# Low-rank decay product of a GLA layer moved out of the kernel's first phase, with row sums per token

## Chip, cores and metric

One core of one Trainium2 chip. The metric is device microseconds of one execution of the whole program, the median of several; lower is better.

## The reference, cut to what matters

Two blocks of layers on x (256 tokens, 1024 features, fp32). Only the entrance of the first block matters here: an RMS norm, one wide product with w_in, whose columns are split among several consumers, and a gated linear attention (GLA) whose decay comes from 16 of these columns (ha) through a second small product.

```python
def rmsnorm(x, g):
    xf = x.astype(jnp.float32)
    y = xf * lax.rsqrt(jnp.mean(xf * xf, axis=-1, keepdims=True) + EPS)
    return (y * g.astype(jnp.float32)).astype(x.dtype)

h = rmsnorm(x, ln1[i])
hq, hk, hv, hr, ha, hatt, hgate = _split_cols(h @ w_in[i], SPLIT_SIZES)
log_a = jax.nn.log_sigmoid((ha @ w_a2[i] + b_a[i]).astype(jnp.float32)) / GLA_TAU
o = gla_mixer(hq.reshape(B, S, GLA_HEADS, GLA_DK), hk.reshape(B, S, GLA_HEADS, GLA_DK),
              hv.reshape(B, S, GLA_HEADS, GLA_DV), log_a.reshape(B, S, GLA_HEADS, GLA_DK))
```

Behind it come dilated attention, gates, an MLP, and a second block with gated feed-forward layers, a convolution and latent attention.

## The kernel before, in words

The program is a list of phases, one for each weight matrix (or part of one). A phase has groups of 256 output columns; a group has blocks of four 128-row pieces of the weight, 512 KB each. SP loads the blocks in order into a ring of eight (`raw`). Each value is held as a high part (rounded to the format that TensorE multiplies at full pace) and the rest: ACT rounds a block five ahead of TensorE (`round_block`, L1006, "cast"), DVE forms the rest four ahead (`rest_block`, L1284), and TensorE multiplies high with high and low (`high`, L606, 512 columns) and low with high (`low`, L612, 256 columns). For x the same two parts lie in `xa`.

The results of group G stand in one of two accumulator banks (`ps`), bank G % 2. Behind a group ACT copies the half with the small terms (`take_lohalf`, L1034, "half copy"), DVE adds it to the other half (L1334, `val`), and only then may TensorE start group G + 2 (`val_done`). DVE scales by the norm afterwards (`keep`), so that the products need not wait for the norm.

Each engine runs its own list, written out by hand in program order: for each group first `ahead` (casts, rests), then the group's evacuation, then the steps that tables put there. `GLA_AT` is such a table: it names behind which group each GLA step runs (z, log, cum, q', kdec, scores, upd0, upd2, o, on0, on1, oT, og), and it holds for TensorE, ACT and DVE alike. Other steps are tied to fixed groups: `angles` (sine and cosine of the positions; DVE at att_k2 group 0, ACT at att_k2 group 1, `sine_and_cosine` on DVE at att_v2 group 0), and `small_inputs` (ACT issues the DMAs of gains and small tables).

Before, the first phase is "ha": 128 columns of w_in of which 16 are used, three products of 256 columns for each piece (L654), as its width is not one of the wide phases. TensorE first transposes x (L690), ACT copies it out (L1142), DVE splits it (`split_gained`, L1299, L1302), ACT squares it (L1050), and TensorE sums the squares over the features with a matrix of ones (`input_sum`, L711). ACT's root and DVE's reciprocal give the norm; then come the issues of `small_inputs` (L1157 to L1164), the groups of gla_q, and behind them the norm turned to one value per token, the gains turned (L690) and the relative bias (L728).

## Time and profile before

| | us |
|---|---|
| median of three runs | 1505.89 |
| lowest, highest | 1505.78, 1507.74 |
| span of the profiled execution | 1504.7 |
| TensorE busy in it | 1483.5 |
| DVE busy | 1139.9 |
| ACT busy | 746.9 |
| GpSimd busy | 39.5 |

The profile is of one execution; its times run from the first to the last instruction, and the runs' time has a little more around it. TensorE's busy time counts matmuls whose ends are modelled, so small waits do not show in it; they are read from the order in time. "PE" is TensorE, "PEld" its weight load, "POOL" GpSimd, and ACTq the issue of a DMA by ACT. A matmul with plain fp32 operands has two records.

### The profile page before, as it was taken

What the parts mean: (1) busy time and instruction counts of PE and PEld (TensorE: products, weight loads), DVE (VectorE), ACT (ScalarE), POOL (GpSimd) and SP (SyncE); (2) the same over time, 40 slices, a digit from 0 to 9 for tenths busy, and PEclk for the clock granted to TensorE, in tenths of its full rate; (3) what the DMA queues carried; (4) which work ended last, traced back from release to release, by engine and by line L of the source; (5) the groups of instructions that cost most, each with busy time, mean ns of one, the idle gap of its engine ahead of it and who ended that gap; (6) DMA issues with size and microseconds to landing.
All of it is one profiled execution on the core that took longest, in us unless ns stands there. A gap on an engine that the chain in (4) does not pass through costs nothing.

```text
span 1504.7 us, 25207 instructions
## 1 busy us (share of the span) xinstructions
PE 1483.5 (99%) x9770; PEld 1331.1 (88%) x9770; DVE 1139.9 (76%) x1521; ACT 746.9 (50%) x1011; POOL 39.5 (3%) x77
## 2 busy tenths in 40 slices
PE   8999999999999999999999999999999999999997
PEld 6889899998898988888986888999888998888887
DVE  6777866789865688787876877678776788887754
ACT  5645456545434375544544645445553444555443
POOL 1000000200000000000121000000000000000000
PEclk9999999999999999999999999999999999999999
DMA  7636665456655566645632666567664664466553
GB/s 224 188 114 180 190 178 159 151 184 191 186 187 190 162 189 184 193 154 186 217 112 66 189 185 193 156 189 217 184 192 155 194 171 154 127 184 192 164 171 113
DMA packets 268919, 260.12 MB, mean 173 GB/s; under 512 B 15702, under 2 KB 267172, under 8 KB 268826
## 3 DMA queue, kind: packets, MB, share of 16 engines
q1 hardware_dynamic: 266832, 255.89, 56.4%
q0 software_dynamic: 1072, 1.98, 0.5%
q8 instruction: 64, 1.05, 0.3%
q10 hardware_dynamic: 922, 0.97, 0.2%
q14 instruction: 29, 0.24, 0.1%
HBM read 257.73 MB, written 1.07 MB: 172 GB/s over the span
## 4 chain that ended last, share of the span: by engine, by line
PE 93%; DVE 4%; ACT 1%; issue 1%; DMA 0%; DVEq 0%; ACTq 0%
PE ps L606 43%; PE ps L612 22%; PE ps L654 22%; PE misc L868 2%; PE misc L690 1%; PE misc L822 1%; PE misc L813 1%; DVE wsplit L1284 0%; PE misc L843 0%; PE misc L686 0%; DVE plain L1360 0%; PE misc L711 0%; DVE val L1334 0%; DMA plain<-in_x_dram 0%; PE misc L772 0%
## 5 line engine op out<-in xcount | busy, mean ns | idle before, releaser
L1284 DVE TENSOR_TENSOR wsplit<-raw,wsplit 128x1024 fp32r<-128x1024 f32 (+2 forms) x532 | 584.7, 1129 | 104.2 <-ACT wsplit L1006 93.9
L1006 ACT CAST wsplit<-raw 128x1024 fp32r<-128x1024 f32 (+2 forms) x532 | 494.5, 968 | 174.8 <-DMA raw<-in_ffn_w_dram 85.1
L606 PE MATMUL ps<-xa,wsplit 128*128 128x512 f32 x1552 | 388.0, 393 | 0.3 <-PE misc L711 0.3
L606 PEld LDWEIGHTS ps<-xa,wsplit 128*128 128x128 f32 x1552 | 284.6, 188 | 58.1 <-issue 1.7
L606 PE MATMUL ps<-parts,wsplit 128*128 128x512 f32 x1068 | 267.4, 393 | 4.4 <-DVE parts L1313 2.8
L606 PEld LDWEIGHTS ps<-parts,wsplit 128*128 128x128 f32 x1068 | 195.4, 189 | 43.0 <-issue 2.0
L1034 ACT COPY lohalf<-ps 128x512 f32<-128x512 f32 x152 | 89.0, 585 | 290.2 <-PE ps L606 235.9
L612 PE MATMUL ps<-xa,wsplit 128*128 128x256 f32 x1552 | 218.1, 282 | 0.0
L1334 DVE TENSOR_TENSOR val<-ps,lohalf 128x512 f32<-128x512 f32 x152 | 105.1, 691 | 144.2 <-ACT lohalf L1034 143.8
L612 PEld LDWEIGHTS ps<-xa,wsplit 128*128 128x128 f32 x1552 | 206.2, 191 | 7.6
L654 PE MATMUL ps<-xa,wsplit 128*128 128x256 f32 x1392 | 174.5, 286 | 0.7 <-DVEq L1329 0.7
L654 PEld LDWEIGHTS ps<-xa,wsplit 128*128 128x128 f32 x1392 | 170.7, 193 | 3.0 <-DVEq L1329 0.9
L654 PE MATMUL ps<-parts,wsplit 128*128 128x256 f32 x1308 | 160.9, 284 | 0.7 <-DVEq L1329 0.7
L654 PEld LDWEIGHTS ps<-parts,wsplit 128*128 128x128 f32 x1308 | 158.9, 192 | 1.7 <-DVEq L1329 0.9
L612 PE MATMUL ps<-parts,wsplit 128*128 128x256 f32 x1068 | 149.2, 283 | 0.0
L612 PEld LDWEIGHTS ps<-parts,wsplit 128*128 128x128 f32 x1068 | 142.7, 192 | 6.2
L1071 ACT ACTIVATE work<-t 128x512 f32<-128x512 f32 x48 | 30.4, 633 | 101.8 <-DVE t L1373 101.8
L1050 ACT ACTIVATE sq<-x 128x512 f32<-128x512 f32 x36 | 22.5, 631 | 66.1 <-DVE x L1445 41.3
L1313 DVE TENSOR_TENSOR parts<-work,parts 128x512 f32 (+1 forms) x64 | 44.3, 693 | 9.3 <-DVE parts L1312 3.9
L606 PE MATMUL ps<-wsplit,xa 128*128 128x512 f32 x160 | 42.9, 393 | 0.0
L606 PEld LDWEIGHTS ps<-wsplit,xa 128*128 128x128 f32 x160 | 29.4, 188 | 5.8
L1312 DVE CAST parts<-work 128x512 f32 (+1 forms) x64 | 27.4, 428 | 7.5 <-DVE work L1397 5.6
(273 smaller groups left out, 988.4 us busy)
## 6 DMA issues: line engine op xcount, KB each, us to landing
raw<-in_ffn_w_dram SPq DMA_DIRECT2D x176, 512.0 KB, 3.8
raw<-in_w_in_dram SPq DMA_DIRECT2D x76, 512.0 KB, 3.7
raw<-in_ffn_w_dram SPq DMA_DIRECT2D x96, 384.0 KB, 3.1
raw<-in_w_mlp_dram SPq DMA_DIRECT2D x64, 512.0 KB, 3.6
raw<-in_conv_w_pw_dram SPq DMA_DIRECT2D x24, 512.0 KB, 3.4
raw<-in_ffn_w_dram SPq DMA_DIRECT2D x32, 256.0 KB, 3.1
raw<-in_w_o_gla_dram SPq DMA_DIRECT2D x8, 512.0 KB, 3.4
raw<-in_w_out_dram SPq DMA_DIRECT2D x8, 512.0 KB, 3.4
```

Source lines behind the costliest of these rows:

```text
L606: return mm(ps[:, bank, c, :], still, both.rearrange("p h t -> p (h t)"), start=p.k0[j] + kk == 0, stop=end, skip_group_check=True)
L612: return mm(ps[:, bank, c, T:2 * T], still, moves, start=False, stop=end, skip_group_check=True)
L654: last = mm(ps[:, bank, c, 0:T], still, moves, start=st and n == 0, stop=en and n == 2, skip_group_check=True)
L868: last = mm(conv_out(i, c)[32 * q:32 * q + 32, :], conv_w(2 * i + c)[:, m, q, :], shifted(i)[:, c, q, 4 * m:4 * m + T], start=(m == 0), st ...
L1006: nc.scalar.copy(wsplit[:, slot, 0:kn, 0, 0:p.width], raw[:, slot, 0:kn, 1, 0:p.width]).then_inc(hi_done, 1)
L1034: nc.scalar.copy(lohalf[:, G % 2, :, :], ps[:, G % 2, :, T:2 * T]).then_inc(lohalf_done, 1)
L1050: act_fn(sq[:, q % 2, :, :], src, ACT.Square).then_inc(squared, 1)
L1071: act_fn(gated[:, :, :], t1[:, :, :], ACT.Silu if kind == "swiglu" else ACT.Sigmoid).then_inc(gate_out, 1)
L1284: TT(wsplit[:, slot, 0:kn, 1, 0:p.width], raw[:, slot, 0:kn, 1, 0:p.width], wsplit[:, slot, 0:kn, 0, 0:p.width].bitcast(F32), ALU.subtract ...
L1312: step(vec.tensor_copy(dst[:, :, 0, :], src))
L1313: TT(dst[:, :, 1, :], src, dst[:, :, 0, :].bitcast(F32), ALU.subtract).then_inc(ready, n)
L1334: TT(val[:, :, :], total, lohalf[:, G % 2, :, :], ALU.add).then_inc(val_done, 1)
```

## The change

- The phase "ha" and its sums by ones are gone. DVE forms the sum of squares of each token from the rows of x in two halves (`square_sum`), ACT takes the root, DVE the reciprocal; a product of ones with a diagonal matrix spreads it over the partitions (`first_rstd`, within gla_q's second group), and DVE copies it to `rstd`.
- x is split from the accumulators: ACT writes the high part with the gain as scale, DVE the rest (`low_input`); ACT copies x itself later (`copy_input`).
- The 16 columns of ha are loaded by an own DMA, into columns of `w_ha` (padded with zeros to 32), scaled by the gain on DVE behind gla_q, and multiplied in plain fp32 behind gla_k's first group: eight pieces, on three column tiles of 32 (`low_rank`). The three partial sums are added by the next product (z), whose weight stands there three times, on 97 of 128 rows.
- Gains and relative bias move from behind gla_q's second group to behind gla_k's first; every GLA step up to on1 and oT moves one group later; the angles stay. `small_inputs` stands at gla_q's first group and has three DMAs more.
- Thirteen transposes of the identity run while TensorE waits for x. GpSimd has two memsets more and two steps less.
- As one group less lies ahead, banks are named by the phases' numbers where they were fixed.

```diff
-GLA_AT = {("gla_k", 0): "z", ("gla_k", 1): "log", ("gla_v", 0): "cum", ("gla_v", 1): "q'", ("gla_v", 2): "kdec",
-          ("gla_v", 3): "scores", ("att_q2", 0): "upd0", ("att_q2", 1): "upd2", ("att_k2", 0): "o",
-          ("att_k2", 1): "on0", ("att_v2", 0): "on1", ("att_v2", 1): "oT", ("att_q0", 0): "og0", ("att_q0", 1): "og1"}
+GLA_AT = {("gla_k", 1): "z", ("gla_v", 0): "log", ("gla_v", 1): "cum", ("gla_v", 2): "q'", ("gla_v", 3): "kdec",
+          ("att_q2", 0): "scores", ("att_q2", 1): "upd0", ("att_k2", 0): "upd2", ("att_k2", 1): "o",
+          ("att_v2", 0): "on0", ("att_v2", 1): "on1", ("hr", 0): "oT", ("att_q0", 0): "og0", ("att_q0", 1): "og1"}
...
-        add("ha", wide(w_in, COL_HA, P), 1, K8, from_xa, ("ha",), width=P)
...
-                    if p.name == "ha":
-                        input_sum(j + 1)
-                if p.name == "ha":
-                    input_sum(3)
+                    if p.name == "gla_q" and g == 1 and j == 0:
+                        first_rstd()
...
+            for _ in range(5):
+                transpose_to(ps[:, 1, 1, 0:P], ident[:, :])
...
+            for _ in range(8):
+                transpose_to(ps[:, 1, 1, 0:P], ident[:, :])
...
-            def input_sum(q):
-
-                pe.wait_ge(squared, q + 1)
-                for c in range(2):
-                    last = mm(misc[:, 3, 0:T], ones[:, :], sq[:, q % 2, c, :], start=(q == 0 and c == 0),
-                              stop=(q == 3 and c == 1), skip_group_check=True)
-                last.then_inc(summed, 1)
-                if q == 3:
-                    pe.wait_ge(summed, 4)
-                    pe.sem_inc(norm_sum, 1)
+            def first_rstd():
+
+                dv_did(pe, "diag")
+                pe.wait_ge(x_copied, 1)
+                for t in range(NT):
+                    last = mm(misc[:, 0, t * P:(t + 1) * P], ones[:, :], diag[:, t, :], start=True, stop=True,
+                              skip_group_check=True)
+                last.then_inc(s_pe, 1)
+
+            def low_rank():
+                dv_did(pe, "ha_w")
+                pe.wait_ge(x_copied, 4)
+                for k in range(NC):
+                    q = 32 * (k % 3)
+                    last = mm(misc[q:q + 32, 3, 0:T], w_ha[:, k, :], x[:, k, :], start=k < 3, stop=k >= NC - 3,
+                              skip_group_check=True)
+                last.then_inc(s_pe, 1)
...
-                        if p.name == "gla_q" and g == 1:
+                        if p.name == "gla_k" and g == 0:
                             pe.wait_ge(s_rows, 16 * (len(GAINS) - 1))
                             transpose_to(gains_turned, gain_rows, GAIN_N).then_inc(s_pe, 1)
+                            low_rank()
...
+            dv_did(act, "ln1")
             for c in range(4):
+                if c >= 2:
+                    round_block(*locate(c - 2), c - 2, None)
                 pe_did(act, f"xT{c}")
+                for k in (2 * c, 2 * c + 1):
+                    last = act_fn(xa[:, k, 0, :], misc[:, c, (k % 2) * T:(k % 2 + 1) * T], ACT.Copy,
+                                  scale=gain[:, k:k + 1])
+                last.then_inc(x_high, 1)
+            round_block(*locate(2), 2, None)
+
+            def copy_input(c):
+
+                act.wait_ge(ready, 2 * c + 2)
                 nc.scalar.copy(x[:, 2 * c:2 * c + 2, :], misc[:, c, :].rearrange("p (k t) -> p k t", k=2)
-                               ).then_inc(new_x, 1)
-            for c in range(4):
-                round_block(*locate(c), c, None)
-                square_pair("w_in", c, x[:, 2 * c:2 * c + 2, :])
+                               ).then_inc(x_copied, 1)
+
+            copy_input(0)
+            act.wait_ge(const_ready, 1)
+            round_block(*locate(3), 3, None)
+            copy_input(1)
+            dv_did(act, "ss")
+            act_fn(root_tok[:, :], half_tok[:, :], ACT.Sqrt, bias=consts[:, 0:1], scale=1.0 / D).then_inc(s_ac, 1)
+            settle()
             round_block(*locate(4), 4, None)
-            act.wait_ge(const_ready, 1)
+            copy_input(2)
+            copy_input(3)
 
             def small_inputs():
 
+                act.dma_start(w_ha[:, :, 0:GLA_RANK], rows(w_in)[:, :, COL_HA:COL_HA + GLA_RANK]).then_inc(s_ha, 16)
                 at = 0
                 for name, n in GAINS:
                     v = a[name]
@@ -1156,8 +1186,9 @@
                     if at:
                         act.dma_start(gain_rows[at:at + n, :], v.rearrange("(c p) -> c p", p=P)).then_inc(s_rows, 16)
...
-                act.dma_start(wa2[0:GLA_RANK, :], a["w_a2"][0]).then_inc(s_setup, 16)
-                act.dma_start(wa2[GLA_RANK:GLA_RANK + 1, :], a["b_a"]).then_inc(s_setup, 16)
+                for q in range(3):
+                    act.dma_start(wa2[32 * q:32 * q + GLA_RANK, :], a["w_a2"][0]).then_inc(s_setup, 16)
+                act.dma_start(wa2[96:97, :], a["b_a"]).then_inc(s_setup, 16)
...
-                            if p.name == "ha":
-                                small_inputs()
+                        if p.name == "gla_q" and g == 0:
+                            small_inputs()
...
-            for c in range(4):
-                v.wait_ge(new_x, c + 1)
+            def square_sum(half):
+
+                v.wait_ge(s_x if half == 0 else s_x2, 16)
+                part = xrow[:, :, half * D // 2:(half + 1) * D // 2]
+                for t in range(NT):
+                    ins = STT(work[:, 2 * t:2 * t + 2, :].rearrange("p a b -> p (a b)"), part[:, t, :], 1.0,
+                              part[:, t, :], ALU.mult, ALU.mult, accum_out=sum_tok[:, t, half:half + 1])
+                step(ins)
+
+            def low_input(c):
+
+                v.wait_ge(x_high, c + 1)
                 after_split()
-                split_gained(xa[:, 2 * c:2 * c + 2, :, :], x[:, 2 * c:2 * c + 2, :], 2 * c, 2)
-                if c == 1:
-                    for s in range(2):
-                        rest_block(*locate(s), s, None)
-            for s in range(2, REST_AHEAD):
-                rest_block(*locate(s), s, None)
+                for k in (2 * c, 2 * c + 1):
+                    STT(xa[:, k, 1, :], misc[:, c, (k % 2) * T:(k % 2 + 1) * T], gain[:, k:k + 1],
+                        xa[:, k, 0, :].bitcast(F32), ALU.mult, ALU.subtract).then_inc(ready, 1)
+                halves[0] += 2
+
+            square_sum(0)
+            low_input(0)
+            low_input(1)
+            rest_block(*locate(0), 0, None)
+            low_input(2)
+            rest_block(*locate(1), 1, None)
+            low_input(3)
+            square_sum(1)
+            done("ss", TT(half_tok[:, :], sum_tok[:, :, 0], sum_tok[:, :, 1], ALU.add))
+            rest_block(*locate(2), 2, None)
+            ac_did(v, "root")
+            step(vec.reciprocal(rstd_tok[:, :], root_tok[:, :]))
+            for t in range(NT):
+                ins = TS(diag[:, t, :], ident[:, :], rstd_tok[:, t:t + 1], None, ALU.mult)
+            done("diag", ins)
+            rest_block(*locate(3), 3, None)
 
...
+                        if p.name == "gla_q" and g == 0:
+                            pe_did(v, "rstd")
+                            step(vec.tensor_copy(rstd[:, :], misc[:, 0, 0:T]))
...
-                            pe_did(v, "gainT")
+                            v.wait_ge(s_ha, 16)
+                            done("ha_w", TT(w_ha, w_ha, gain[:, 0:NC].unsqueeze(2).to_broadcast([P, NC, 32]), ALU.mult))
+                        if p.name == "gla_k" and g == 0:
+                            pe_did(v, "ha")
                             done("gain", vec.tensor_copy(gain[:, NC:GAIN_N], gains_turned[:, NC:GAIN_N]))
+                            done("ha", TT(ha[0:96, :], misc[0:96, 3, 0:T], rstd[0:96, :], ALU.mult))
```

ACT's list around `small_inputs`: before, from the DMA of w_a2 to the half copy of gla_q's first group.

```order
L1159 DMA sbias<-in_w_a_dram 16x512
L1160 DMA sbias<-in_b_a_dram 1x512
L1161 DMA t<-in_rel_bias_dram 32x12
L1162 DMA work<-in_bias_c_dram 33x1152
L1163 DMA ropec<-in_rope_c_dram 128x129
L1164 DMA t<-in_positions_dram 128x256
L1006 CAST wsplit<-raw 128x4x256 x2
L1034 COPY lohalf<-ps 128x512
```

The same place now.

```order
L1190 DMA sbias<-in_w_a_dram 16x512 x3
L1191 DMA sbias<-in_b_a_dram 1x512
L1192 DMA t<-in_rel_bias_dram 32x12
L1193 DMA work<-in_bias_c_dram 33x1152
L1194 DMA ropec<-in_rope_c_dram 128x129
L1195 DMA t<-in_positions_dram 128x256
L1045 COPY lohalf<-ps 128x512
```

The half copy of that group stands directly behind the issues now, and two casts of blocks ahead behind it; three DMAs of w_a2 stand where one was, and one more (w_ha, not shown) leads the list.

ACT's list behind the GLA step "o" (the squares, L1112 before, L1123 now): before, in att_k2's two groups.

```order
L1112 ACTIVATE plain,stat<-misc 128x256 x8
L1116 ACT_TABLE_LOAD
L1116 ACTIVATE stat<-stat,consts 128x8
L1006 CAST wsplit<-raw 128x4x256 x2
L1034 COPY lohalf<-ps 128x512
L1168 ACT_TABLE_LOAD
L1168 ACTIVATE sin<-gained 128x256
L1169 ACTIVATE cos<-gained,consts 128x256
L1006 CAST wsplit<-raw 128x4x256 x2
L1034 COPY lohalf<-ps 128x512
```

Now, at the end of att_k2's second group and in att_v2.

```order
L1123 ACTIVATE plain,stat<-misc 128x256 x8
L1127 ACT_TABLE_LOAD
L1127 ACTIVATE stat<-stat,consts 128x8
L1199 ACT_TABLE_LOAD
L1199 ACTIVATE sin<-gained 128x256
L1200 ACTIVATE cos<-gained,consts 128x256
L1017 CAST wsplit<-raw 128x4x256 x2
L1045 COPY lohalf<-ps 128x512
L1017 CAST wsplit<-raw 128x4x256 x2
L1045 COPY lohalf<-ps 128x512
```

Sine and cosine (L1168, L1169 before; L1199, L1200 now) moved ahead of the casts and the half copy that stand behind "o".

DVE's list from on0 to on1 (L1565 before, L1594 now): before.

```order
L1565 TENSOR_SCALAR plain<-misc,stat 128x256 x4
L1284 TENSOR_TENSOR wsplit<-raw,wsplit 128x4x256 x2
L1334 TENSOR_TENSOR val<-ps,lohalf 128x512
L1360 TENSOR_SCALAR extra<-val,rstd_tok 128x256 x2
L1565 TENSOR_SCALAR plain<-misc,stat 128x256 x4
L1665 SCALAR_TENSOR_TENSOR val<-sin,cos 128x256
L1666 TENSOR_TENSOR val<-sin 128x256
L1667 TENSOR_SCALAR cos<-val 128x256
L1668 COPY sin<-val 128x256
L1284 TENSOR_TENSOR wsplit<-raw,wsplit 128x4x256 x2
```

Now.

```order
L1594 TENSOR_SCALAR plain<-misc,stat 128x256 x4
L1719 SCALAR_TENSOR_TENSOR val<-sin,cos 128x256
L1720 TENSOR_TENSOR val<-sin 128x256
L1721 TENSOR_SCALAR cos<-val 128x256
L1722 COPY sin<-val 128x256
L1315 TENSOR_TENSOR wsplit<-raw,wsplit 128x4x256 x2
L1365 TENSOR_TENSOR val<-ps,lohalf 128x512
L1388 TENSOR_SCALAR extra<-val,rstd_tok 128x256 x2
L1594 TENSOR_SCALAR plain<-misc,stat 128x256 x4
```

"Sine and cosine" (four steps of 128x256) stood behind on1 and stands between on0 and on1 now.

## Rows read from the trace of the kernel before

**Rows 1.** The page: engine totals (part 1) and the chain by engine (part 4).
```profile
PE 1483.5 (99%) x9770; PEld 1331.1 (88%) x9770; DVE 1139.9 (76%) x1521; ACT 746.9 (50%) x1011; POOL 39.5 (3%) x77
...
PE 93%; DVE 4%; ACT 1%; issue 1%; DMA 0%; DVEq 0%; ACTq 0%
```

**Rows 2.** Waits of TensorE in the whole span: total, times, longest.
```profile
PE ps L606 <- DVE parts L1313: 2.8, 2, 1.6
```

**Rows 3.** Timeline, TensorE, 4 to 34 us: start, us, engine, line, operation, tiles, count.
```profile
4.84 3.67 PE L690 MATMUL misc<-ident,plain 128*128 128x128 f32 x16 [2.12 <-DMA plain<-in_x_dram]
...
10.33 2.04 PE L711 MATMUL misc<-sq,ones 128*128 128x256 f32 x4 [1.81 <-ACT sq L1050]
...
18.88 2.08 PE L606 MATMUL ps<-xa,wsplit 128*128 128x512 f32 x8 [0.30 <-PE misc L711]
...
30.25 0.28 PE L690 MATMUL misc<-ident,root 1*128 1x1 f32 x2
...
32.73 1.66 PE L606 MATMUL ps<-xa,wsplit 128*128 128x512 f32 x6
```

**Rows 4.** Busy time by stretch: engines, then granted clock, DMA share, GB/s.
```profile
0.00:10.00 10.00, 3.92 (x17) 3.45 (x17) 3.29 (x10) 4.69 (x8) 4.39 (x26) 1.00 0.82 256
...
10.00:16.20 6.20, 5.87 (x28) 5.43 (x29) 5.79 (x12) 4.41 (x8) 0.00 (x0) 1.00 1.10 348
```

**Rows 5.** Timeline, ACT and its DMA issues, 15 to 27 us.
```profile
16.05 2.92 ACT L1006 CAST wsplit<-raw 128x1024 fp32r<-128x1024 f32 x3
...
18.71 0.29 ACTq L1157 DMA_DIRECT2D logit<-in_ln_dram  x1
...
25.23 0.50 ACTq L1164 DMA_DIRECT2D t<-in_positions_dram  x1
...
25.77 2.00 ACT L1006 CAST wsplit<-raw 128x1024 fp32r<-128x1024 f32 x2 [6.42 <-issue]
```

**Rows 6.** Groups by form, 0 to 170 us: the half copy and the sum.
```profile
L1034 ACT COPY lohalf<-ps 128x512 f32<-128x512 f32 x21 | 12.3, 584 | 45.5 <-PE ps L612 24.9 <-PE ps L606 20.4
...
L1334 DVE TENSOR_TENSOR val<-ps,lohalf 128x512 f32<-128x512 f32 x21 | 14.5, 690 | 14.7 <-ACT lohalf L1034 14.6
```

**Rows 7.** Groups, TensorE, 755.8 to 762.9 us: the convolution's products.
```profile
L868 PE MATMUL misc<-plain 128*32 128x256 f32 x128 | 7.1, 379 | 0.0
```

**Rows 8.** Timeline and busy time (with granted clock), around 812 us.
```profile
808.64 3.62 PE L966 MATMUL ps<-cos,ones 128*128 128x256 f32 x16
...
813.91 1.30 PE L606 MATMUL ps<-parts,wsplit 128*128 128x512 f32 x4 [1.65 <-DVE parts L1313]
...
816.34 2.07 PE L606 MATMUL ps<-parts,wsplit 128*128 128x512 f32 x4 [1.13 <-DVE parts L1313]
...
812.30:816.10 3.80, 1.30 (x4) 0.59 (x4) 3.56 (x8) 2.35 (x6) 0.00 (x0) 1.00 0.00 0
...
816.10:819.40 3.30, 3.06 (x10) 2.68 (x11) 3.06 (x8) 2.33 (x4) 0.00 (x0) 0.50 0.00 0
```

**Rows 9.** Timeline, TensorE, 98 to 121 us: product after "o"; oT.
```profile
102.44 2.11 PE L606 MATMUL ps<-xa,wsplit 128*128 128x512 f32 x8
...
119.32 1.91 PE L690 MATMUL misc<-ident,plain 128*128 128x128 f32 x16
```

**Rows 10.** Timeline, ACT, 105 to 121 us.
```profile
109.12 0.58 ACT L1034 COPY lohalf<-ps 128x512 f32<-128x512 f32 x1
...
109.71 1.28 ACT L1168 ACT_TABLE_LOAD   x1
...
111.86 2.00 ACT L1006 CAST wsplit<-raw 128x1024 fp32r<-128x1024 f32 x2
```

**Rows 11.** Timeline, DVE, 105 to 121 us.
```profile
108.30 1.23 DVE L1284 TENSOR_TENSOR wsplit<-raw,wsplit 128x1024 fp32r<-128x1024 f32 x1 [6.30 <-ACT wsplit L1006]
...
116.77 1.66 DVE L1565 TENSOR_SCALAR plain<-misc,stat 128x256 f32<-128x256 f32 x4
...
120.04 1.23 DVE L1284 TENSOR_TENSOR wsplit<-raw,wsplit 128x1024 fp32r<-128x1024 f32 x1
```

More of the change, by code:

```diff
@@ L344, in program @@
             nlow += sum(p.halves(g) for g in range(p.groups))
-            nkept += p.groups if p.evac[0] in ("ha", "keep", "keep_tok") else 0
+            nkept += p.groups if p.evac[0] in ("keep", "keep_tok") else 0
             nblk += p.groups * len(p.kns)
@@ L365, in program @@
         norms, pairs, new_x_at, sums, told = {}, {}, {}, 0, 0
-        for name, n in (("w_in", 4), ("mlp1", 4), ("w_pg", 4), ("ln_f", 4), ("ffn1_up0", 4), ("pw1", 4), ("conv", 4),
+        for name, n in (("mlp1", 4), ("w_pg", 4), ("ln_f", 4), ("ffn1_up0", 4), ("pw1", 4), ("conv", 4),
                         ("ffn2_up0", 4), ("ffn1_up1", 4), ("mla_a", 4), ("cq", 2), ("ckv", 1), ("ffn2_up1", 4)):
@@ L413, in program @@
         gain_row = flat(60, 4)
+        xrow = flat(0, 8).rearrange("p (t n) -> p t n", t=NT)
+        diag = sq[:, 0, :, 0:P]
         def bias_of(h, t):
@@ L477, in program @@
         ident_ready = sem("ident_ready")
+        x_high = sem("x_high")
+        x_copied = sem("x_copied")
+        s_ha = sem("s_ha")
         s_ln1 = sem("s_ln1")
@@ L503, in program @@
                    + heads(("qk", 0), ("pT", 2), ("pv", 3)) + ["ffn2_up1.tokT", "xtok0", "xtok1"])
-        name_steps("dv", ["ln1", "gain", "rel", "z", "abs", "log", "b", "blast", "gla_in", "attn"]
-                   + ["st0", "st1", "st2", "trig", "on0", "on1", "setup", "og"]
+        name_steps("dv", ["ln1", "ss", "diag", "ha_w", "gain", "ha", "rel", "z", "abs", "log", "b", "blast", "gla_in", "attn"]
+                   + ["st0", "st1", "st2", "trig", "on0", "setup", "on1", "og"]
                    + [f"att{h}.{s}" for h in range(ATT_H) for s in ("max", "norm", "o")]
@@ L509, in program @@
                    + heads(("max", 0), ("norm", 1)) + ["outsum", "out"])
-        name_steps("ac", ["log", "expb", "expd", "ktok", "o", "oroot", "trig"]
+        name_steps("ac", ["root", "log", "expb", "expd", "ktok", "o", "oroot", "trig"]
                    + [f"att{h}.{s}" for h in range(ATT_H) for s in ("exp", "pT")]
@@ L734, in gla_step @@
                 if k == "z":
-                    pe.wait_ge(kept, 1)
                     dv_did(pe, "rel")
                     for t in range(NT):
-                        last = mm(misc[:, t, :], ha[0:GLA_RANK + 1, t * P:(t + 1) * P], wa2,
+                        last = mm(misc[:, t, :], ha[:, t * P:(t + 1) * P], wa2,
                                   start=True, stop=True)
@@ L835, in attend @@
                     ac_did(pe, f"{name}.pT")
-                    o = misc[:, 3, 0:T] if ng > 1 else ps[:, 0, par % 2, 0:T]
+                    o = misc[:, 3, 0:T] if ng > 1 else ps[:, 1 - by["w_o"].group0 % 2, par % 2, 0:T]
                     for g in range(ng):
@@ L927, in _ @@
                             query_turns()
-                        if g == 0 and p.name in norm_at and p.name != "ha":
+                        if g == 0 and p.name in norm_at:
                             norm_sum_step(norm_at[p.name])
@@ L965, in _ @@
                     for _ in range(8):
-                        mm(ps[:, 1, 1, 0:T], ones[:, :], cos[:, :], start=True, stop=True, skip_group_check=True)
+                        mm(ps[:, by["pw1"].group0 % 2, 1, 0:T], ones[:, :], cos[:, :], start=True, stop=True, skip_group_check=True)
                 if p.name == "mla_kr":
@@ L1339, in evacuate @@
                     after_split()
-                if kind == "ha":
-                    keep(p, g, TT(ha[0:GLA_RANK, :], total[0:GLA_RANK, 0, :], rstd[0:GLA_RANK, :], ALU.mult))
-                    taken()
                 if kind == "keep":
@@ L1487, in add_squares @@
                     v.wait_ge(squared, q + n)
+                if (c == 2 or c == n == 1) and norms[name]:
+                    v.wait_ge(norm_sum, norms[name])
                 if c == 2 or c == n == 1:
-                    v.wait_ge(norm_sum, norms[name])
                     v.wait_ge(squared, q + min(n, 2))
@@ L1614, in head_out @@
                 pe_did(v, f"mla{h}.pv")
-                split(parts[:, h:h + 1, :, :], ps[:, 0, h % 2:h % 2 + 1, 0:T], 1)
+                split(parts[:, h:h + 1, :, :], ps[:, 1 - by["w_o"].group0 % 2, h % 2:h % 2 + 1, 0:T], 1)
             def rope_keys():
@@ L1809, in _ @@
             pl.sem_inc(ident_ready, 1)
-            step(gp.memset(flip[:, :], 0.0))
-            step(gp.affine_select(out=flip[:, :], in_=flip[:, :], compare_op=ALU.not_equal, fill=1.0,
-                                  base=1 - P, pattern=[[1, P]], channel_multiplier=1))
             step(gp.memset(relrow[REL_BUCKETS:REL_BUCKETS + 1, :], 1.0))
@@ L1821, in _ @@
             step(gp.memset(ha, 1.0))
+            step(gp.memset(wa2, 0.0))
+            step(gp.memset(w_ha, 0.0))
             step(gp.memset(tri[:, :], 1.0 / 16.0))
@@ L1884, in _ @@
                     shift_copies(1)
-                if name == "w_in":
-                    continue
-                pl.wait_ge(norm_sum, norms[name])
-                if name not in ("w_in", "conv"):
+                if norms[name]:
+                    pl.wait_ge(norm_sum, norms[name])
+                if name != "conv":
                     continue
```

22 lines of the change are left out of this document (9 added, 13 removed).

## The prediction

> **What bounds the kernel now.** I read the page first: TensorE is busy 99% of the span and the chain that ended last is 93% TensorE [rows 1]. So a stretch is worth what it takes out of TensorE's own line, or what it makes TensorE wait. Then I read TensorE's waits: the ones inside the program are single ones of 1 to 3 us [rows 2]; nothing recurring is there to win. Last I read TensorE in order of time at the start [rows 3]. It transposes x at 4.84, sums squares and runs the low-rank group from 10.33, starts gla_q at 18.88, does the small products (root per token, gains, relative bias) from 30.25 to 32.73 and starts gla_k there. Only the stretch before 18.88, the small products and the GLA steps that move can change. Behind them every engine does what it did.
>
> **The start of gla_q.** Gone are the ha phase (24 products of 256 columns) and eight sums by ones. The first gla_q product now waits for the first two split chunks of x and the first cast block. ACT takes x from the accumulators as soon as the first four transposes are through, near 6.0 us; four halves and one cast of 1.0 us (three take 2.92 [rows 5]) bring it to 8.8, and DVE's splits end there too. So gla_q starts some 10 us earlier. This is not what is gained, because of the next point.
>
> **ACT's DMA issues are now in the way.** While ACT issues the small DMAs it starts nothing else: it sat idle 6.42 us before the cast at 25.77, and 17 issues ran from 18.71 to 25.73 [rows 5]. In the old order the small product of ha was read by DVE alone, and TensorE had two gla_q groups to work on meanwhile. In the new order ACT's half copy of gla_q's first group stands behind 20 issues, and gla_k may not start before DVE has added that group up, since there are two banks. The chain, step by step:
> - The issues stand behind the casts of blocks 5 and 6, so block 6 must have landed. x and seven blocks are 9 x 524 KB = 4.72 MB; the DMAs moved 2.56 MB by 10 us and 348 GB/s after it [rows 4], so 2.16 MB more take 6.2 us: 16.2 us. (DVE's sums of squares and ACT's root, on which the fourth cast waits, are done by 15.5 in the same way of counting.)
> - 20 issues at 7.02/17 = 0.41 us: 8.3 us, to 24.5.
> - Half copy 0.58, sum 0.69 [rows 6], 0.1 between them: gla_k starts at 25.9.
> TensorE reaches that point at about 21.3 (8.8, two groups in the 11.4 us that they took from 18.88 to 30.25 [rows 3], 0.6 for a late rest, 0.5 for the diagonal products), so it stands idle 4.6 us. That gla_q starts 10 us or 8 us earlier is then worth nothing: the wait hides it, and hides the thirteen added transposes, whether they help or not.
> Against 32.73 before, gla_k starts 6.8 us earlier. But 2.3 of the 2.5 us of small products (30.25 to 32.73) now stand behind gla_k's first group, and the low-rank products come with them. Their price: 64 products of 32 output columns took 7.1 us in the convolution [rows 7] (two records each), 0.44 per four side by side. Eight on three column tiles are three rounds, 1.3 us; one after another they would be 8 x 0.44 = 3.5. I take 1.3, since the row is the same kind. The sum for the start: 6.8 - 2.3 - 1.3 = **3.2 us gained** (between 1.0 with products in a row and 3.9 if the issues start at 15.5). The product z has more rows and the same columns, and costs what it did.
> The page TensorEngine Tiling of the Trainium skill (Key Properties) speaks against the small tiles: it says that a change of the tiling mode drains the array. It gives no price; the convolution row above holds few changes in many products, so a price for one does not show, and the sum leaves it at nothing.
>
> **The clock.** TensorE's granted clock fell once in this trace: after the eight filler products ended at 812.2 TensorE had 1.65 us idle, a burst of four products and 1.13 us idle, and from 816.1 to 819.4 the record shows 0.50, the lower level of 1.2 GHz [rows 8]. Four products of 512 columns took 2.07 there. Idle 4.6 us is longer than that whole stretch, so the clock falls behind the new wait, and about 3.1 us of work go at half speed: **1.55 us lost** (nothing at the least, 1.65 at the most).
>
> **The GLA steps, one group later each.** From z to "o" each step keeps its distance in groups from the one before it, on all three engines, so the small waits there stay. But the angles do not move with them. Before, ACT's work after "o" was eight squares and a root, then casts and the half copy at 109.12, and only then sine and cosine, 109.71 to 111.86 [rows 10]. Now "o" and the angles stand behind the same group: sine and cosine come before the casts, and push the next half copy back by 2.1 us. On DVE "sine and cosine" (118.43 to 120.04) stood behind on1 [rows 11]; now it stands between on0 and on1 and adds 1.6. Before, on1 was done at 118.43, 16.0 us after "o" ended at 102.44, and oT started at 119.32, 16.9 after it, without a wait [rows 9, 11]. Now on1 is done 16.0 + 2.1 + 1.6 = 19.7 us after "o" plus 0.1, and oT stands again three groups behind "o", 16.7: TensorE waits **3.1 us** (2.2 if the gaps between these rows close, 3.5 with what else queues on DVE). Nothing hides it: what is behind oT on TensorE is the next group of hr.
>
> **Small edits.** The squares per token on DVE, ACT's split from accumulators and the rest are inside the first 21 us, under the wait for ACT. The weight of the low-rank product is scaled on DVE just before TensorE wants it (about 30.8 against 31.5); 0.5 us at most if its DMA of 64-byte rows is late. Parities and GpSimd's memsets cost nothing: GpSimd is busy 39.5 us of 1505.
>
> **Sum.** -3.2 + 1.55 + 3.1 = +1.45 us. The profiled span of 1504.7 becomes 1506.2; the three times shown have their median at 1505.89, so 1507.3. What can be told from no change here is about 0.2%, 3.0 us. So my forecast is: no change that can be told, rather a little slower. The change buys time at the start and pays it back twice.
>
> **Rivals.**
> - *The clock falls behind the second wait too* (slower). TensorE then has idle 3.1 us and oT, whose sixteen transposes come next. In the trace the fall came 3.9 us after dense work ended [rows 8], and 3.1 idle plus part of oT is the same length; from there it decides. Sixteen transposes at the start took 3.67 us [rows 3] against 1.91 for oT's [rows 9], so at half speed they cost 1.8 more, and the hr group behind them 1.55. That gives 1507.3 + 3.4 = 1510.7, or 1508.9 if the clock rises during the transposes. Against it: the wait alone is shorter than 3.9. Chance 0.26.
> - The same by a page: TensorE: Matmul & The Clock Gate (Part 4) in the Trainium skill says that the full clock does not engage in transpose mode. By that rule, the trace agrees as far as it goes: sixteen transposes over 3.67 us kept the pace of half speed to the end, and only after the products from 10.33 on did eight products of 512 columns take 2.08 [rows 3], half of the pace at 816.34. By that rule oT would not bring the clock back, and the time would be 1510.7.
> - *No wait before oT* (no change, or faster). If DVE makes up the 3.7 us, the rest is -3.2 + 1.55: 1504.2, and 1502.7 if the first fall is missing too. DVE had 6.30 us idle before 108.30 [rows 11], but that lies before on0, not behind it, so it does not help. Chance 0.24, half of it at 1502.7.
> - *The first fall is missing, the second wait is there*: 1505.8. Chance 0.1.
> - *The issues wait for the casts to be finished, not only given out.* At 18.71 the first issue came before the cast row ended at 18.97 [rows 5], so ACT gives out ahead by at least one. If not by five, the issues start at 19.7 instead of 16.2, gla_k 3.5 later: 1510.8. Chance 0.05.
> - *The change does not do what it says*: the low-rank products run in a row for 3.5 us instead of side by side, 1509.5. Chance 0.05.
> - The forecast itself has 0.3.
>
> **Range and chances.** 1502.7 to 1510.8 reaches from the case without the second wait and without a fall to the one with both falls, and takes in the bounds of the start (1.0 to 3.9 gained) and of the second wait (2.2 to 3.5) around the forecast; two unlucky ends together fall outside. Slower by over 0.2% (above 1508.9): 0.22 of the first rival's 0.26 and the two small ones, 0.32. Faster by over 0.2% (below 1502.9): half of the case without the wait and 0.03 for a start better than its bound, 0.15. The rest, 0.53, is within 0.2%.
>
> **What would show it.** In the new profile: TensorE idle 4 to 5 us before gla_k's first product, released by DVE's sum (val), with ACT idle over 7 us behind its issues; the granted clock at 0.5 just behind it; a wait of 3 us before the sixteen transposes of oT, released by DVE's TENSOR_SCALAR on misc. The first gla_q product near 9 us. Low-rank products in 1.3 us. I am wrong if gla_k starts before 24 us, if oT has no wait, or if TensorE's line from hr's second group on is not the old one shifted.

## The result and the profile after

| | before | after |
|---|---|---|
| median, us | 1505.89 | 1510.1 |
| lowest, highest | 1504.32, 1507.74 | 1506.57, 1511.8 |
| runs | 21 | 21 |
| span of the profiled execution | 1504.7 | 1506.9 (its time 1508.68) |

The ratio is 1.0023 with a 95% interval of 1.0017 to 1.0029: the change makes the kernel slower by 0.23%. That is little, but the interval does not reach 1. After's runs fall in two groups with nothing between them: ten from 1506.6 to 1508.7 (median 1508.0) and eleven from 1510.1 to 1511.8 (median 1510.65). The profiled execution is of the lower group. I take it apart first and come to the upper one with the experiments.

First the waits of TensorE in after (total, times, longest), which answer to [rows 2]:

```profile
PE ps L609 <- DVE val L1365: 5.8, 1, 5.8
...
PE misc L691 <- DVE plain L1594: 2.6, 1, 2.6
```

Both are new: one behind gla_q's second group, one before the transposes oT. Then TensorE in order of time (start, busy us, line, operation, tiles, count), which answers to [rows 3, 9]:

```profile
4.90 2.62 PE L691 MATMUL misc<-ident,plain 128*128 128x128 f32 x16
9.08 2.08 PE L609 MATMUL ps<-xa,wsplit 128*128 128x512 f32 x8 [1.56 <-ACT wsplit L1017]
...
27.16 3.49 PE L609 MATMUL ps<-xa,wsplit 128*128 128x512 f32 x8 [5.83 <-DVE val L1365]
...
34.26 0.26 PE L691 MATMUL misc<-ident,logit 110*128 110x110 f32 x1
34.45 1.49 PE L725 MATMUL misc<-x,taps 128*32 128x256 f32 x16
35.87 2.10 PE L739 MATMUL misc<-work,t 33*4 33x384 f32 x6
37.90 2.11 PE L609 MATMUL ps<-xa,wsplit 128*128 128x512 f32 x8
...
44.92 2.41 PE L609 MATMUL ps<-wsplit,xa 128*128 128x512 f32 x8
...
107.46 2.11 PE L609 MATMUL ps<-wsplit,xa 128*128 128x512 f32 x8
...
118.77 1.98 PE L609 MATMUL ps<-xa,wsplit 128*128 128x512 f32 x8
...
127.13 1.97 PE L691 MATMUL misc<-ident,plain 128*128 128x128 f32 x16 [2.60 <-DVE plain L1594]
128.85 2.10 PE L609 MATMUL ps<-xa,wsplit 128*128 128x512 f32 x8
```

gla_q starts at 9.08, not 18.88, and gla_k at 27.16, not 32.73 [rows 3]. The low-rank products take 1.42 us (34.45 to 35.87). The balance against the kernel before can be struck at four places where both kernels start the same group (the small GLA product z stands ahead of gla_v's start in both):

| start of | before | after | gained so far |
|---|---|---|---|
| gla_k, first group | 32.73 | 27.16 | 5.57 |
| gla_v, first group | 46.14 | 44.92 | 1.22 |
| hr, first group | 120.98 | 118.77 | 2.21, less 1.66 for oT, which before has already done: 0.55 |
| hr, second group | 126.67 | 128.85 | -2.18 |

From the last row on both lines are the same; the spans differ by 2.2. The 5.57 shrink to 1.22 by what now stands behind gla_k's first group (34.26 to 37.90, 3.64 us) and by the clock, whose record is 0.50 from 23.3 to 30.1 and which costs 1.3; z gives 0.6 back. The columns behind the stretch are the busy us of TensorE, its weight load, DVE, ACT and GpSimd, then the granted clock:

```profile
20.00:23.30 3.30, 1.33 (x6) 0.75 (x4) 0.08 (x1) 0.00 (x0) 0.00 (x0) 1.00 1.16 279
23.30:30.10 6.80, 2.94 (x7) 2.37 (x8) 3.62 (x4) 4.37 (x6) 0.00 (x0) 0.50 0.45 132
...
124.40:127.10 2.70, 0.12 (x2) 0.00 (x0) 2.60 (x7) 1.87 (x2) 0.00 (x0) 1.00 0.64 181
127.10:131.00 3.90, 3.87 (x26) 3.53 (x27) 3.82 (x5) 0.17 (x1) 0.00 (x0) 1.00 0.12 41
```

Here the clock fell within the first wait, 2.0 us after TensorE's last product (its group ends at 21.33), and not behind the second wait. That ACT's issues cause the first wait stands in ACT's order of time:

```profile
16.96 0.42 ACTq L1181 DMA_DIRECT2D taps<-in_w_in_dram  x1
...
17.59 1.05 ACT L1017 CAST wsplit<-raw 128x1024 fp32r<-128x1024 f32 x1
...
21.67 2.04 ACTq L1190 DMA_DIRECT2D sbias<-in_w_a_dram  x3
...
25.24 0.45 ACTq L1195 DMA_DIRECT2D t<-in_positions_dram  x1
25.73 0.59 ACT L1045 COPY lohalf<-ps 128x512 f32<-128x512 f32 x1 [7.10 <-issue]
```

Twenty issues fill 16.96 to 25.69, and the half copy on which DVE's sum and then gla_k depend comes right behind them. The second wait is seen on DVE: sine and cosine (120.19 to 121.73) stand between the first and the second norm, which ends at 127.08.

```profile
118.50 1.66 DVE L1594 TENSOR_SCALAR plain<-misc,stat 128x256 f32<-128x256 f32 x4
120.19 0.42 DVE L1719 SCALAR_TENSOR_TENSOR val<-sin,cos 128x256 f32<-128x256 f32 x1
...
125.42 1.66 DVE L1594 TENSOR_SCALAR plain<-misc,stat 128x256 f32<-128x256 f32 x4
```

### The profile page after: what moved, and what is told of

Read it like the earlier page. It is cut to its first block, busy times and chain, and to the rows that moved or that the text cites. A ratio compares the mean times of both kernels' runs of the same rounds, so it can differ in the third digit from the quotient of the medians.

```text
span 1506.9 us, 25182 instructions
## 1 busy us (share of the span) xinstructions
PE 1480.5 (98%) x9761; PEld 1327.5 (88%) x9761; DVE 1138.6 (76%) x1523; ACT 746.7 (50%) x1013; POOL 40.7 (3%) x77
## 3 DMA queue, kind: packets, MB, share of 16 engines
q0 software_dynamic: 1072, 1.98, 0.6%
## 4 chain that ended last, share of the span: by engine, by line
PE 91%; DVE 4%; issue 2%; ACT 2%; DMA 0%; ACTq 0%; SPq 0%; DVEq 0%
PE ps L609 42%; PE ps L615 22%; PE ps L657 21%; PE misc L878 2%; PE misc L691 1%; DVE wsplit L1315 1%; PE misc L832 1%; ACT wsplit L1017 1%; PE misc L823 0%; DMA raw<-in_w_in_dram 0%; PE misc L853 0%; DVE plain L1388 0%; DVE val L1365 0%; PE misc L687 0%; PE misc L782 0%
## 5 line engine op out<-in xcount | busy, mean ns | idle before, releaser
L615 PE MATMUL ps<-xa,wsplit 128*128 128x256 f32 x1552 | 218.3, 283 | 0.0
L657 PE MATMUL ps<-xa,wsplit 128*128 128x256 f32 x1368 | 170.0, 284 | 0.7 <-DVEq L1360 0.7
```

The costliest lines, as they stand in the source:

```text
L615: return mm(ps[:, bank, c, T:2 * T], still, moves, start=False, stop=end, skip_group_check=True)
L657: last = mm(ps[:, bank, c, 0:T], still, moves, start=st and n == 0, stop=en and n == 2, skip_group_check=True)
```

## The experiments

All are edits of after. Where a median is compared with before, it is with runs of before on the same chip (medians 1505.8 to 1506.1).

**1. The issues on SP.** Nineteen small transfers (all but the one-hot table's) go to SP's queue, ahead of weight block 8.

```diff
 (load, on SP)
+                if s0 == RING:
+                    small_inputs()
                 if s0 >= RING:
                     sp.wait_ge(used, lin(s0 - RING + 1, RING, i))
```

> The changed kernel, with nineteen of the twenty small DMAs issued by SP between its block 7 and block 8 (gains first, the rest once GpSimd has cleared their places); ACT issues only the bias table. Theory: the 5.8 us wait before gla_k is ACT's half copy standing behind its issues, and the clock falls because of it. Then the wait goes, gla_k starts near 21.4, the granted clock stays at 1.00 there, and 5.8 + 1.6 = 7.4 us go against the changed kernel: about 1502.7. The wait of 2.6 us before oT stays. Rival: the next thing is late just behind it (the blocks behind SP's issues, the scaled weight of the low-rank product, DVE's rests), the wait moves to the low-rank products or to gla_k's second group, and less than half of the 7.4 is gained: 1506.5 or more.

Measured: 1506.41 (1503.96 to 1511.55, 12 runs), ratio to before 1.0011 (1.0000 to 1.0022). The wait of 5.8 us is gone, and gla_k's first group follows gla_q at full pace, but a new wait takes half of the gain back, and the clock fell behind it in this profile (0.51 from 30.2 to 33.7; the low-rank products took 2.77 us, not 1.49). TensorE's waits:

```profile
PE misc L745 <- DVE taps L1803: 3.1, 1, 3.1
...
PE misc L711 <- DVE plain L1600: 2.6, 1, 2.6
```

ACT shows where it starts; the bracket is the idle time ahead and what ended it:

```profile
26.74 1.05 ACT L1037 CAST wsplit<-raw 128x1024 fp32r<-128x1024 f32 x1 [6.60 <-DMA raw<-in_w_in_dram]
27.70 0.58 ACT L1065 COPY lohalf<-ps 128x512 f32<-128x512 f32 x1
```

Block 8, issued behind the small transfers at 21.09, was not there before 26.7. The half copy stands behind its cast, and on DVE the scaling of the low-rank weights (29.76) stands behind the sum and the product of that group. So the expectation missed my edit's own cost: SP's queue carries the weights. This profile also shows the second fall of the clock, which after's own does not:

```profile
124.54 2.47 PE L711 MATMUL misc<-ident,plain 128*128 128x128 f32 x16 [2.61 <-DVE plain L1600]
126.66 3.30 PE L629 MATMUL ps<-xa,wsplit 128*128 128x512 f32 x8
...
126.00:129.80 3.80, 3.80 (x14) 3.16 (x12) 3.40 (x4) 1.56 (x3) 0.00 (x0) 0.57 0.01 2
```

Behind the same wait of 2.6 us oT starts at full clock. The record falls at 125.9, 1.3 us into oT and 3.9 us after the last product (121.9), and is near 0.5 until 129.3. oT takes 2.47 and not 1.97, and the eight products 3.30 and not 2.10: 1.7 us.

**2. The angles behind both norms.** ACT's sine and cosine, and DVE's part of them, one group later.

```diff
-                   + ["st0", "st1", "st2", "trig", "on0", "setup", "on1", "og"]
+                   + ["st0", "st1", "st2", "trig", "on0", "on1", "setup", "og"]
 (ACT)
-                        if p.name == "att_k2" and g == 1:
+                        if p.name == "att_v2" and g == 0:
                             angles()
 (DVE)
-                        if p.name == "att_v2" and g == 0:
+                        if p.name == "att_v2" and g == 1:
                             sine_and_cosine()
```

> The changed kernel, with the angles moved one group later as the GLA steps were: ACT's sine and cosine in att_v2's first group, DVE's sine-and-cosine behind on1. Theory: the wait before oT is made by these two, so it falls from 2.6 us to under 0.5, and what the clock loses behind it in a part of the runs goes too: the median falls by 2.6 to 5 us, to 1505 to 1507.5, and the runs no longer spread over 5 us. The start stays: gla_k at 27.2, clock low behind it. Rival: DVE is late in any case because on0 and on1 stand in the same groups as keep_tok, the wait stays over 1.5 us, the median within 1 us of 1510.

Measured: 1505.71 (1504.54 to 1506.26, 11 runs), ratio 0.9998 (0.9990 to 1.0007). The wait before oT is gone, and so is the upper group: the spread is 1.7 us where after has 5.2. The norm's last row now ends at 123.47, a microsecond before TensorE wants it at 124.47:

```profile
121.81 1.66 DVE L1594 TENSOR_SCALAR plain<-misc,stat 128x256 f32<-128x256 f32 x4
123.51 0.42 DVE L1719 SCALAR_TENSOR_TENSOR val<-sin,cos 128x256 f32<-128x256 f32 x1
```

This one move takes back all that the change had cost: 1510.1 to 1505.7. The first wait, with its fall of the clock, is still there (5.5 us in this profile), so it is not what makes the upper group.

**3. Both moves.**

> Both edits together. Theory: both payments go, 7.4 + 2.6 in the profile and the spread of the clock: 1498 to 1500.5, faster than the kernel before by 5.5 to 8 us. Rival (the waits are not independent: TensorE, once early, meets the next late engine in the GLA steps): the sum is smaller than that of the two single edits by over 2 us.

Measured: 1503.89 (1500.16 to 1507.59, 12 runs), ratio 0.9986 (0.9975 to 0.9996). Better than before, but 3.4 to 5.9 us above what I expected. The profiled execution (1503.33) shows two reasons: the wait for the scaled low-rank weights is 3.4 us here, by the block that is late (the record is 1.00 behind it, so no fall comes with it), and the fall of the clock near 816 us, which the kernel before has too, is twice as long as there and costs 2.5 us (last section). The two single edits had gained 3.7 and 4.4 us, both together 6.2, 1.9 less; the rival had asked for over 2.

**4. The issues behind the half copy.** They stay on ACT, but `small_inputs()` is called after `evacuate(p, g, None, 0)` of gla_q's first group, not ahead of it.

> The changed kernel, with ACT's half copy of gla_q's first group ahead of its twenty issues instead of behind them. Theory: the issues then hold up the next thing on ACT: gla_k starts near 21.4 without a wait, but casts 7 and 8 and the half copy of gla_q's second group come behind the issues (near 30.5), DVE scales the low-rank weight near 32.5, and TensorE waits 5 us before the low-rank products, which start near 32.7 instead of 34.4. The clock falls there too. Gain 1.5 to 2 us: about 1508.3. Rival: the half copy of the first group alone was the trouble, the issues hide behind gla_k's first group, and most of 7.4 us is gained: 1503 to 1504.

Measured: 1505.42 (1503.79 to 1511.25, 12 runs), ratio 1.0003 (0.9994 to 1.0012), between the expectation and its rival. The first wait is gone; a wait of 2.5 us for the scaled low-rank weights stands in its place, behind which the clock did not fall in this profile (1.00 from 27.1 to 31). DVE's order tells why:

```profile
21.66 1.23 DVE L1315 TENSOR_TENSOR wsplit<-raw,wsplit 128x1024 fp32r<-128x1024 f32 x1
26.28 1.22 DVE L1315 TENSOR_TENSOR wsplit<-raw,wsplit 128x1024 fp32r<-128x1024 f32 x1 [3.40 <-ACT wsplit L1017]
27.71 0.69 DVE L1365 TENSOR_TENSOR val<-ps,lohalf 128x512 f32<-128x512 f32 x1 [0.21 <-ACT lohalf L1045]
28.44 0.69 DVE L1374 SCALAR_TENSOR_TENSOR plain<-val,rstd 128x512 f32<-128x512 f32 x1
29.16 0.42 DVE L1797 TENSOR_TENSOR taps<-taps,gain 128x256 f32<-128x256 f32 x1
```

DVE is idle 3.4 us for a cast, while the scaling that TensorE wants at 27.1 stands behind it.

**5. The scaling one group earlier too.** To run 4 this is added:

```diff
-                        if p.name == "gla_q" and g == 1:
+                        if p.name == "gla_q" and g == 0:
                             v.wait_ge(s_ha, 16)
                             done("ha_w", TT(w_ha, w_ha, ...
```

> After, with two edits: the 20 small transfers are issued on ACT behind the half copy of gla_q's first group (as in half_copy_first), and the scaling of the low-rank weights (DVE, 0.42 us) stands behind the first group of gla_q instead of the second. In half_copy_first TensorE waited 2.5 us for that scaling, which DVE reached only at 29.2 us behind the half copy, the sum and the product of the second group (27.7, 28.4). Theory (a wait that moved, and goes with its cause): the 2.5 us go and the low-rank products start near 27.1 us; the lowest runs fall from 1503.8 to about 1501.3, the median from 1505.4 to about 1503, unless the weight blocks of gla_k, cast behind the issues, are late next: then half of it comes back as a wait at L609 and the median is about 1504.3. The wait of 2.6 us before oT stays. Rival (the wait was of the transfers' landing, not of DVE's order): nothing is gained, 1505.4.

Measured: 1502.42 (1501.69 to 1506.04, 9 runs), ratio 0.9981 (0.9971 to 0.9991). The lowest runs fell by 2.1 and the median by 3.0; the low-rank products no longer wait, and the next thing late is a transfer, 0.5 us.

**6. Runs 2 and 5 together.**

> scale_before_half together with angles_later (sine and cosine prepared behind the two norms of the linear attention's output). Theory: the 2.5 us at the low-rank products and the 2.6 us before oT both go, and with no wait over 2 us in the first 130 us of TensorE the clock has no reason to fall there: median 1499.5 to 1501, and the spread of the runs is below 2 us but for the falls late in the kernel that every version has. If the blocks of gla_k are late next, 1501 to 1502.5. Rival (the falls are random and do not hang on waits): the spread stays at 7 us, as in both_moves (1500.2 to 1507.6).

Measured: 1499.41 (1497.21 to 1502.47, 6 runs), ratio 0.9962 (0.9950 to 0.9973). As expected. In TensorE's order nothing is left of either wait:

```profile
26.85 0.26 PE L691 MATMUL misc<-ident,logit 110*128 110x110 f32 x1
27.04 1.49 PE L725 MATMUL misc<-x,taps 128*32 128x256 f32 x16
29.26 2.10 PE L739 MATMUL misc<-work,t 33*4 33x384 f32 x6 [0.72 <-DMA t<-in_positions_dram]
31.28 2.12 PE L609 MATMUL ps<-xa,wsplit 128*128 128x512 f32 x8
```

The spread is 5.3 us and not the under 2 us that I expected.

> three_moves once more, for its interval and as the partner of the next run on the same chip. Theory: median 1498.5 to 1500.5, most runs between 1497 and 1501. Rival (the six runs of the first time were a lucky draw of a spread of 7 us, as in both_moves): median above 1501.5.

Measured: 1500.56 (1497.47 to 1502.57, 6 runs), ratio 0.9968 (0.9956 to 0.9981), just over the expected 1500.5 and under the rival's 1501.5. The twelve runs of both times have their median at 1499.9: some 6 us below the kernel before (0.38 and 0.32% by the two ratios) and 10 below after.

**7. Work in the second wait.** Twenty transposes of the identity, whose results are overwritten, ahead of oT's.

```diff
                 if k == "oT":
+                    dv_did(pe, "on0")
+                    for _ in range(20):
+                        transpose_to(misc_flat[:, 0:P], ident[:, :])
                     dv_did(pe, "on1")
```

> After, with 20 identity transposes (128x128, about 0.1 us each, 2.1 us in all) ahead of oT's transposes, in the 2.6 us in which TensorE waits there for the second norm; their results are overwritten. Nothing else is changed, and the wait itself (until 127.1 us) stays. Theory (the upper half of after's runs, 1510.1 to 1511.8, are those in which the clock fell behind this wait, and the lower half, 1506.6 to 1508.7, those in which it did not): with TensorE busy the clock does not fall, the upper group is gone, the median is 1507.3 to 1508 and no or hardly any run lies above 1509.5. Rival (the two groups come from somewhere else, from the first wait or from late in the kernel): they stay, and the median is 1510 as for after.

Measured: 1508.15 (1507.05 to 1509.36, 11 runs), ratio 1.0015 (1.0006 to 1.0024). DVE is as late as in after, TensorE only isn't idle:

```profile
125.03 2.35 PE L691 MATMUL misc<-ident 128*128 128x128 f32 x20
127.79 1.97 PE L691 MATMUL misc<-ident,plain 128*128 128x128 f32 x16 [0.41 <-DVE plain L1597]
```

The upper group is gone: none of eleven runs is above 1509.4, where eleven of after's 21 are above 1510. So the upper group comes from TensorE being idle there, as distinct from DVE being late. That it is the clock which falls in those executions is not seen directly, as no profile of an upper run of after was taken. For it speak run 1's profile and the mean granted clock of after's runs: 0.995 to 0.997 in the lower group, 0.994 in eight and 0.995 in three of the eleven upper ones.

**8. Without the identity transposes** of the first 5 us (5 and 8 of them).

> After, without the 13 transposes of the identity in the first 5 us, which compute nothing that is used. Theory (they keep TensorE busy, so that its clock has risen by the time the rows of x arrive): the 16 transposes of x take about 3.7 us as in the kernel before, not 2.6 us, end near 8.5 us instead of 7.7, and the first products run at half rate for some us: the chain is 1.5 to 3.5 us longer, median 1511.5 to 1513.5. Rival (transposes do not raise the clock, or the first weight blocks are late anyway): no difference, 1510.

Measured: 1510.44 (1506.63 to 1510.76, 7 runs), ratio 1.0030 (1.0019 to 1.0041): no difference from after's 1510.1, the rival's number. The theory was half right:

```profile
4.87 3.68 PE L691 MATMUL misc<-ident,plain 128*128 128x128 f32 x16 [2.25 <-DMA plain<-in_x_dram]
9.05 2.28 PE L609 MATMUL ps<-xa,wsplit 128*128 128x512 f32 x8 [0.51 <-issue]
```

The transposes of x are slower, 3.68 for 2.62, and end near 8.5, but the first product waits for casts and starts at 9.05 all the same; only 0.2 us is lost in it. The same without a wait behind it that could hide a loss:

> three_moves without the 13 identity transposes of the first 5 us. In no_identity_transposes the 16 transposes of x took 3.68 us instead of 2.62, and yet the first product of gla_q started at 9.05 us (9.08 in after) and took 2.28 us (2.08), since it waits for casts and splits and not for the transposes. There a wait of 5 us behind gla_q would have hidden a loss; here nothing hides one. Theory (the transposes gain nothing that counts): 0.2 us from the first product's rows is all that can come, median within 0.7 us of three_moves_again. Rival (the wait hid a loss, the identity transposes pay where TensorE is dense behind them): 1 to 2.5 us slower than three_moves_again.

Measured: 1499.86 (1497.65 to 1502.21, 5 runs), ratio 0.9957 (0.9944 to 0.9971). The identity transposes gain nothing that can be measured, though with five and six runs that spread over 5 us a gain of half a microsecond would not show.

## Why the prediction was right, and where it was not

**The start.** The chain of ACT's issues was right in kind and short by 1.26 us: gla_k at 27.16, forecast 25.9. The issues began at 16.96 (16.2), took 8.73 us (8.3; three issues of one table's 16 rows each took 0.68), and the copy and the sum behind them 1.5 with the gaps (1.4). That the wait hides the earlier gla_q is seen in gla_q starting 9.8 us earlier and gla_k only 5.57. The thirteen transposes need no wait to hide them: in run 8 the first product starts at the same time without them. TensorE's idle time was 5.83 (4.6).

**The small products.** 3.64 us now stand behind gla_k's first group; the sum had 2.3 + 1.3. The low-rank products took 1.42 for the estimated 1.3, eight on three column tiles side by side. The rival of products in a row (3.5 us) falls. The page TensorEngine Tiling of the Trainium skill (Key Properties) says that a change of the tiling mode drains the array; so far as 1.42 against 1.3 goes, that is worth some 0.1 us here.

**The first fall of the clock.** The eight products took 3.49 for 2.11, and the group from 27.16 to 34.26 took 7.10, where before's (32.73 to 38.55) took 5.82: 1.3 to 1.4 lost, forecast 1.55. "z costs what it did" was slightly off: it took 1.32 us of TensorE's line where before took 1.91, and gave 0.4 back in the product behind it (2.41 for 1.98). The product of the cumulated sums (step "cum") now waits 0.34 us, which it did not before, although the forecast said that the small waits among the GLA steps stay. With that the start had gained 0.55 by the first group of hr; the forecast's 3.2 - 1.55 was 1.65. This is the term that was mis-sized in the lower group, by 1.1 us, and gla_k's start, 1.26 late, is what did it.

**The wait before oT.** The second norm was done 19.6 us after the product behind "o" (107.46 to 127.08), forecast 19.7. TensorE came to it 17.1 after, not 16.7 (the row of the kernel before had 16.9), so the wait was 2.60 for 3.1. Run 2, which takes the cause away, confirms it. With oT's row and the gaps it cost 2.7.

**The sum** was +1.45; the profiled spans differ by +2.2, and after's lower group has its median at 1508.0 for the 1507.3 forecast.

**The second fall.** What decided the median is the first rival: in a little over half of the runs the clock falls behind the second wait too. I gave it 0.26 and held against it that a wait of 3.1 us is shorter than the 3.9 us of [rows 8]. That comparison is the step that failed. It rests on one single fall, and 3.9 us is no least length: within after's first wait the record fell 2.0 us after the last product. And where the second fall was caught, in run 1's profile, it came 1.3 us into oT and not within the wait, so the wait alone was the wrong thing to compare; the rival itself had counted part of oT in. Run 7 shows that the upper group goes when TensorE is kept busy.

The rival's price, 3.4 us, was too high: the groups' medians are 2.7 apart, and the one fall that a profile caught cost 1.7 us. The mean granted clocks of the two groups, 0.9959 and 0.9943, differ by 0.0016; over 1508 us that is some 5 us more at the lower level in an upper run, 2.5 us of work by my estimate, where run 1's fall lasted 3.4 us. That points to more than one such fall over a lower run, or to a longer one. Which it is stays open, since no profile of an upper run of after was taken.

**How near it came.** The forecast was no change that can be told, rather a little slower. The ratio stands 0.23% above, just past the 0.2% that I took as the bound. The forecast's own case, with one new fall, gave 1507.3, and the lower group has 1508.0; the rival's 1510.7 lies close to the upper group's 1510.65. That last agreement is in part luck: the start was 0.7 too good in it and the price of the second fall 0.7 too high.

Two readings in the prediction were wrong, without an effect on its sum. In the rival on the page's rule the eight products of 18.88 took half of the time of those at 816.34 and so ran at twice their pace, not at half. And the clock of the kernel before did not fall only once: the record is 0.50 in the last 2.5 us of the span too, where TensorE has nothing left to do.

The rule of the page TensorE: Matmul & The Clock Gate of the Trainium skill (Part 4), that the full clock does not engage in transpose mode, is not borne out, if that is the mode of this kernel's transposes, which the trace does not name. In after the sixteen transposes of x, with nothing but transposes ahead of them, took 2.62 us; in the kernel before they took 3.67 [rows 3], and oT's, at full pace, 1.91 [rows 9]. So the pace rose among transposes, although the granted clock in the record is 1.00 over that whole stretch and does not show it.

The other rivals fall: there is a wait before oT, and the issues began while casts were still under way (16.96 against a cast at 17.59).

## What to carry to other kernels

When work is moved to an earlier place, look at what else stands in the queues that it is moved past: here the DMA issues on ACT (17 before, 20 now) had been harmless only because nothing behind them was wanted yet, and sine and cosine only because a norm stood ahead of them. Both costs went with a change of order alone, 6 us below the kernel before in the end, and each wait that was removed uncovered the next one in another engine's queue (late block, then scaling, then a transfer). A queue that carries weights is no free place for small transfers.

## What the runs showed of the hardware

- The same wait of 2.6 us let the granted clock fall in some executions and not in others (1.00 behind it in after's profile, 0.52 from 126.0 to 129.4 in that of run 1), which makes two groups of times out of one kernel.
- The length of a wait did not decide it. All four profiles with a first wait of 5.0 to 6.2 us (after and runs 2, 7 and 8) show a fall. Of the waits before the low-rank products, that of 3.1 us (run 1) has one, and those of 3.4 (run 3) and 2.5 us (run 4) have none.
- A fall also came without such a wait: in run 5's profile the record is 0.50 from 32 to 35 us, behind the small products of 27 to 31 us with 0.5 us of idle time among them. In run 6's profile, with the same order and 0.72 us idle, it did not come, and in that of three_moves_no_identity, with 1.2 us idle, it came again. So waits of 2.6 us are not all that the remaining spread of 5 us comes from.
- The fall near 816 us [rows 8] is not in every execution either, so it can make up a part of the spread, of the kernel before too. Of the twelve profiles seven have it and five do not (those of run 1, of no_identity_transposes and of the three kernels with all three moves). From the second four products to the next whole group it took 4.90 us without a fall (three_moves), 6.23 with the one of the kernel before, and 7.35 in run 3's profile (both_moves), where the record is 0.55 from 811 to 818. The rows, in this order:

```profile
809.56 1.20 PE L609 MATMUL ps<-parts,wsplit 128*128 128x512 f32 x4 [1.13 <-DVE parts L1344]
...
814.46 2.03 PE L609 MATMUL ps<-parts,wsplit 128*128 128x512 f32 x8
...
816.34 2.07 PE L606 MATMUL ps<-parts,wsplit 128*128 128x512 f32 x4 [1.13 <-DVE parts L1313]
...
822.57 1.99 PE L606 MATMUL ps<-parts,wsplit 128*128 128x512 f32 x8
...
811.65 2.08 PE L629 MATMUL ps<-parts,wsplit 128*128 128x512 f32 x4 [1.12 <-DVE parts L1350]
...
819.00 2.03 PE L629 MATMUL ps<-parts,wsplit 128*128 128x512 f32 x8
```

- Three issues of the same small table took 2.04 us on ACT in one profile, 1.38 in another and 1.50 on SP; most other issues took 0.3 to 0.5.
